# First loads in pieces, later waits for the layer norm's parameters, and a last layer norm shared by ScalarE and VectorE

## The reference

```python
proj = h @ w_in                                   # one combined input projection
a_out = dsa_attention(...)                        # indexer, top-256 keys, latent attention
m_out = mlstm(...)                                # chunkwise matrix memory
mix = concatenate([a_out, m_out]) @ w_out
h = layer_norm(DN_ALPHA * h + mix, ln1_g, ln1_b)
ffn = moe(h, ...)                                 # top-4 of 32 experts, clamped SwiGLU
h = layer_norm(DN_ALPHA * h + ffn, ln2_g, ln2_b)

def layer_norm(x, g, b):
    mu = x.mean(-1, keepdims=True)
    var = square(x - mu).mean(-1, keepdims=True)
    return (x - mu) * rsqrt(var + LN_EPS) * g + b
```

## Time and profile before

| | us |
|---|---|
| median of 3 runs | 2545.79 |
| lowest and highest | 2544.07, 2550.18 |
| the profiled execution, its time | 2546.15 |
| the profiled execution, its span | 2544.3 |
| TensorE busy in the span | 2334.9 (92%) |
| VectorE busy | 1778.5 (70%) |
| ScalarE busy | 1397.7 (55%) |
| GpSimd busy | 301.8 (12%) |

### The profile page before, as it was taken

One profiled execution on the slowest core, in us unless ns is written; L12 is line 12 of the kernel. 1 busy time (PEld: TensorE's weight loads), 2 busy tenths in 40 slices (PEclk: granted clock), 3 DMA queues, 4 the chain that ended last, 5 costly groups with the idle time before them and its releaser, 6 DMA issues.

```text
span 2544.3 us, 37381 instructions
## 1 busy us (share of the span) xinstructions
PE 2334.9 (92%) x10580; PEld 1664.2 (65%) x10581; DVE 1778.5 (70%) x3337; ACT 1397.7 (55%) x2081; POOL 301.8 (12%) x233
## 2 busy tenths in 40 slices
PE   7999998789796699999999999999999999999990
PEld 3544448468453277777777777777777777777770
DVE  0387785446235566787987789787969969778795
ACT  0268624555111155566766577565757757556672
POOL 0000931100200000010011011010001101001002
PEclk9999999799898599999999999999999999999995
DMA  4100002000203356687987789686969969768684
GB/s 165 67 5 33 1 21 96 1 1 1 91 1 141 142 192 217 215 294 230 350 297 260 256 284 360 230 298 213 358 221 324 343 208 352 244 218 293 213 288 155
DMA packets 79981, 488.48 MB, mean 192 GB/s; under 512 B 12019, under 2 KB 13299, under 8 KB 28790
## 3 DMA queue, kind: packets, MB, share of 16 engines
q1 hardware_dynamic: 66512, 449.67, 49.3%
q0 software_dynamic: 11440, 34.10, 6.0%
q10 hardware_dynamic: 1974, 4.02, 0.5%
HBM read 461.91 MB, written 33.29 MB: 195 GB/s over the span
## 4 chain that ended last, share of the span: by engine, by line
PE 71%; DVE 15%; issue 6%; ACT 3%; DVEq 2%; DMA 2%; POOL 0%; POOLq 0%; ACTq 0%; SPq 0%
PE ps L792 9%; PE ps L793 9%; PE ps L794 9%; DVE wlo L1595 8%; PE ps L534 7%; PE ps L789 6%; PE ps L790 6%; PE ps L545 5%; PE ps L713 4%; PE ps L813 3%; PE ps L695 2%; DVEq L380 2%; PE ps L824 1%; PE ps L676 1%; PE ps L563 1%
## 5 line engine op out<-in xcount | busy, mean ns | idle before, releaser
L1595 DVE TENSOR_TENSOR wlo<-raw,whi 128x1024 fp32r<-128x1024 f32 x776 | 932.2, 1220 | 208.3 <-ACT whi L1082 168.2
L1082 ACT ACTIVATE whi<-raw 128x1024 fp32r<-128x1024 f32 x776 | 817.6, 1059 | 405.3 <-PE ps L794 372.3
L792 PE MATMUL ps<-whi,xhi 128*128 128x512 f32 x1024 | 418.0, 408 | 0.0
L793 PE MATMUL ps<-wlo,xhi 128*128 128x512 f32 x1024 | 404.7, 395 | 0.0
L794 PE MATMUL ps<-whi,xlo 128*128 128x512 f32 x1024 | 402.6, 393 | 0.0
L792 PEld LDWEIGHTS ps<-whi,xhi 128*128 128x128 f32 x1024 | 194.3, 190 | 66.6 <-issue 27.6
L794 PEld LDWEIGHTS ps<-whi,xlo 128*128 128x128 f32 x1024 | 195.0, 190 | 42.3
L793 PEld LDWEIGHTS ps<-wlo,xhi 128*128 128x128 f32 x1024 | 195.0, 190 | 36.2
L792 PE MATMUL ps<-whi,hhi 128*128 128x512 f32 x512 | 210.3, 411 | 0.0
L1809 POOL DMA_INDIRECT acc<-ysb,idx_cur x45 | 70.6, 1569 | 1140.5 <-DVE ysb L1644 656.5
L794 PE MATMUL ps<-whi,hlo 128*128 128x512 f32 x512 | 201.4, 393 | 0.0
(11 more groups left out here) (337 smaller groups left out, 3348.5 us busy)
## 6 DMA issues: line engine op xcount, KB each, us to landing
raw<-in_w_gu SPq DMA_DIRECT2D x260, 1024.0 KB, 5.3
raw<-in_w_dn SPq DMA_DIRECT2D x128, 1024.0 KB, 5.1
xT<-in_xT SPq DMA_DIRECT2D x2, 2048.0 KB, 15.7
raw<-in_w_out SPq DMA_DIRECT2D x2, 2048.0 KB, 11.1
h1all<-in_x SPq DMA_DIRECT2D x4, 1024.0 KB, 9.0
hext<-h1all SPq DMA_DIRECT2D x8, 512.0 KB, 11.6
acc<-accst SPq DMA_DIRECT2D x8, 512.0 KB, 2.6
fin<-acc SPq DMA_DIRECT2D x2, 2048.0 KB, 13.3
```

Source lines behind the costliest of these rows:

```text
L792: pe.matmul(bank_ap, hi, whi[:, slot, col, :], start=start, stop=False)
L793: pe.matmul(bank_ap, hi, wlo[:, slot, col, :], start=False, stop=False)
L1082: act.activation(whi[:, j % 2, 2 * g:2 * g + 2, :], raw[:, (j + 2) % 3, 2 * g:2 * g + 2, :], ACT.Copy)\
L1595: dve.tensor_tensor(wlo[:, j % 2, s, :], raw[:, (j + 2) % 3, s, :], whi[:, j % 2, s, :].bitcast(f32), ALU.subtract).then_inc(lo_done, 1)
```

## The change

- The first half of `xT` and slab 0 are loaded in four pieces of two `k` each, alternately, on SP's queue, with a semaphore for each piece (`first_in[0..2]`, and for the last piece `x_in[0]` and `raw_in[0]`). TensorE runs the first half of the query product with `k` outside and `m` inside, four banks open at once, and waits for a piece at every second `k`. It waits for the constants only ahead of the first transpose that uses them. ScalarE's queue issues the constants and the small loads after the first piece has landed.
- TensorE waits for `lnp_in` at the first router product, VectorE at the first use of the first layer norm's scale.
- The last layer norm's scale and shift have buffers of their own, free during the expert loop, and are loaded just ahead of it. `gu` becomes half as large, since its second half was not used, and makes room for one of them.
- `fin` is loaded in four DMAs of two tiles. Tiles 0 and 1 take their statistics on VectorE as before. For tiles 2 to 7 ScalarE sums the row, scales it to minus the mean, sums the squares of the difference, and takes the root. VectorE then does two passes on every tile: (x + minus mean) times scale, and that times the reciprocal root, plus shift. GpSimd does nothing there.

```diff
@@ sync
-            sp.dma_start(xT[:, :, 0:512], a["xT"][:, :, 0:512]).then_inc(x_in[0], 16)
-            slab(0, a["w_qi"])
+            for c in range(4):
+                ks = slice(2 * c, 2 * c + 2)
+                sp.dma_start(xT[:, ks, 0:512], a["xT"][:, ks, 0:512]).then_inc(first_in[c] if c < 3 else x_in[0], 16)
+                sp.dma_start(raw[:, 0, ks, :], a["w_qi"][:, ks, :]).then_inc(first_in[c] if c < 3 else raw_in[0], 16)
...
-            for g in range(2):
-                sp.dma_start(fin[:, 4 * g:4 * g + 4, :],
-                             acc[g * 512:(g + 1) * 512, :].rearrange("(t p) d -> p t d", p=P)).then_inc(fin_in[g], 16)
+            for g in range(4):
+                sp.dma_start(fin[:, 2 * g:2 * g + 2, :],
+                             acc[g * 256:(g + 1) * 256, :].rearrange("(t p) d -> p t d", p=P)).then_inc(fin_in[g], 16)
@@ tensor
-            pe.wait_ge(consts_in, 32)
-            feature_major("qi", 0)
+            for k in range(KT):
+                if k in (0, 2, 4):
+                    pe.wait_ge(first_in[k // 2], 32)
+                elif k == 6:
+                    pe.wait_ge(x_in[0], 16)
+                    slab_ready(0)
+                for m in range(4):
+                    if k == 0:
+                        opened(("qi", m, 0))
+                    ins = pe.matmul(bank(("qi", m, 0))[:, :], raw[:, 0, k, m * P:(m + 1) * P], xT[:, k, 0:512],
+                                    start=k == 0, stop=k == KT - 1)
+                    if k == KT - 1:
+                        closes(ins, ("qi", m, 0))
+            feature_major("qi", 0, [(m, 1) for m in range(4)])
...
             b = opened(("grow",))
+            pe.wait_ge(consts_in, 32)
...
+                if t == 0:
+                    pe.wait_ge(lnp_in, 80)
                 for k in range(KT):
                     ins = pe.matmul(b[0:NE, 0:P], w_rt[:, k, :], h1T[:, t % 2, k, :], start=k == 0, stop=k == KT - 1)
...
-            pe.wait_ge(lnp_in, 80)
             for t in range(NT):
                 mix(t)
@@ scalar
+            act.wait_ge(first_in[0], 32)
             act.dma_start(consts[:, :], a["consts"]).then_inc(consts_in, 16)
...
+            for n in range(2):
+                act.wait_ge(acc_out[n], 8 * NT)
+            act.wait_ge(h_out, 16 * NT)
+            act.dma_start(lnq_g[:, :], a["ln2_g"].partition_broadcast(P)).then_inc(lnq_in, 16)
+            act.dma_start(lnq_b[:, :], a["ln2_b"].partition_broadcast(P)).then_inc(lnq_in, 16)
             with act.Fori(0, n_items) as i:
...
-            piece_split(act, n_items, 1, 3)
-            act.wait_ge(all_added, 1)
             act.wait_ge(bgu_in, n_items * 16 + 16)
-            act.dma_start(lnq[:, 0, :], a["ln2_g"].partition_broadcast(P)).then_inc(lnq_in, 16)
-            act.dma_start(lnq[:, 1, :], a["ln2_b"].partition_broadcast(P)).then_inc(lnq_in, 16)
-            for t in range(NT):
+            for t in range(2):
                 act.wait_ge(f_var, t + 1)
                 act.activation(frs[:, 0, t:t + 1], fmv[:, t, 1:2], ACT.Sqrt, bias=consts[:, C_COL + 1:C_COL + 2])\
                    .then_inc(f_root, 1)
-                act.wait_ge(f_sb, t + 1)
-                act.activation(fin[:, t, :], fin[:, t, :], ACT.Identity, scale=frs[:, 0, t:t + 1],
-                               bias=frs[:, 1, t:t + 1]).then_inc(f_norm, 1)
+            step = serial(act, f_sum)
+            for t in range(2, NT):
+                act.wait_ge(fin_in[t // 2], 16)
+                step(act.activation(fdump[:, :], fin[:, t, :], ACT.Copy, accum_out=fmv[:, t, 0:1]))
+                step(act.activation(frs[:, 1, t:t + 1], fmv[:, t, 0:1], ACT.Copy, scale=-1.0 / D))
+                step(act.activation(fdump[:, :], fin[:, t, :], ACT.Square, bias=frs[:, 1, t:t + 1],
+                                    accum_out=fmv[:, t, 1:2]))
+                act.activation(frs[:, 0, t:t + 1], fmv[:, t, 1:2], ACT.Sqrt, scale=1.0 / D,
+                               bias=consts[:, C_COL + 1:C_COL + 2]).then_inc(f_root, 1)
@@ vector
+                if t == 0:
+                    dve.wait_ge(lnp_in, 80)
                 lstep(dve.tensor_tensor(h1all[:, t, :], h1all[:, t, :], lnp[:, 0, :], ALU.mult))
...
             dve.wait_ge(xres_in, 64)
-            dve.wait_ge(lnp_in, 80)
...
-            for t in range(NT + 2):
-                if t < NT:
-                    dve.wait_ge(fin_in[t // 4], 16)
-                    for n in range(2):
-                        fs(dve.bn_stats(fstat[:, t, n, :], fin[:, t, n * 512:(n + 1) * 512]))
-                    dve.bn_aggr(fmv[:, t, :], fstat[:, t, :, :].rearrange("p a b -> p (a b)")).then_inc(f_var, 1)
...
+            for t in range(2):
+                dve.wait_ge(fin_in[t // 2], 16)
+                for n in range(2):
+                    fs(dve.bn_stats(fstat[:, t, n, :], fin[:, t, n * 512:(n + 1) * 512]))
+                dve.bn_aggr(fmv[:, t, :], fstat[:, t, :, :].rearrange("p a b -> p (a b)")).then_inc(f_var, 1)
+            dve.wait_ge(f_var, 2)
+            for t in range(NT):
                 dve.wait_ge(f_root, t + 1)
                 fs(dve.reciprocal(frs[:, 0, t:t + 1], frs[:, 0, t:t + 1]))
+                mean, op = (fmv[:, t, 0:1], ALU.subtract) if t < 2 else (frs[:, 1, t:t + 1], ALU.add)
+                fs(dve.scalar_tensor_tensor(out=fin[:, t, :], in0=fin[:, t, :], scalar=mean, in1=lnq_g[:, :],
+                                            op0=op, op1=ALU.mult))
+                dve.scalar_tensor_tensor(out=fin[:, t, :], in0=fin[:, t, :], scalar=frs[:, 0, t:t + 1], in1=lnq_b[:, :],
+                                         op0=ALU.mult, op1=ALU.add).then_inc(f_done, 1)
```

More of the change, by code:

```diff
@@ L240, in layer_kernel @@
         tail_ones = at("tail_ones", 57.75, [P, P], bf16)
-        gu = at("gu", X + 92.5, [P, 2, 2, SLAB])
+        gu = at("gu", X + 92.5, [P, 2, SLAB])
         brow = at("brow", X + 134.5, [3, 2 * D], bf16)
@@ L254, in layer_kernel @@
         fin = at("fin", X + 102, [P, NT, D])
-        lnq = at("lnq", X, [P, 2, D])
+        fdump = at("fdump", X, [P, D])
+        lnq_g = at("lnq_g", X + 60, [P, D])
+        lnq_b = at("lnq_b", X + 96.5, [P, D])
         fstat = at("fstat", X + 8, [P, NT, 2, 6])
@@ L312, in layer_kernel @@
         x_in = [sem(f"x_in{n}") for n in range(2)]
+        first_in = [sem(f"first_in{c}") for c in range(3)]
         raw_in = [sem(f"raw_in{n}") for n in range(3)]
@@ L364, in layer_kernel @@
         xg_set, all_added = sem("xg_set"), sem("all_added")
-        fin_in, f_step, f_var, f_root, f_sb, f_norm, f_done, f_out = (
-            [sem(f"fin_in{n}") for n in range(2)], sem("f_step"), sem("f_var"), sem("f_root"), sem("f_sb"), sem("f_norm"),
-            {"dve": sem("f_done_dve"), "pool": sem("f_done_pool")}, sem("f_out"))
-        f_shift = ["dve" if t % 3 == 2 else "pool" for t in range(NT)]
-        f_gain = sem("f_gain")
+        fin_in, f_step, f_var, f_root, f_sum, f_done, f_out = (
+            [sem(f"fin_in{n}") for n in range(4)], sem("f_step"), sem("f_var"), sem("f_root"), sem("f_sum"),
+            sem("f_done"), sem("f_out"))
         last_use = [("qi", 3, 1), ("small", 3), ("qa", 3, 1), ("u", 3, 1), ("v", NT - 1), ("z", NT - 1),
@@ L502, in _ @@
             sp.wait_ge(all_added, 1)
[L503 to L505 removed]
+            for g in range(4):
+                sp.dma_start(fin[:, 2 * g:2 * g + 2, :],
+                             acc[g * 256:(g + 1) * 256, :].rearrange("(t p) d -> p t d", p=P)).then_inc(fin_in[g], 16)
             for t in range(NT):
[L507 removed]
+                sp.wait_ge(f_done, t + 1)
                 sp.dma_start(out[0, t * P:(t + 1) * P, :], fin[:, t, :]).then_inc(f_out, 16)
@@ L1611, in swiglu @@
                 n, uses = gu_place(0, quarter, i, n1, blocks)
-                h, up = hb[:, 0, quarter * 256:(quarter + 1) * 256], gu[:, 0, quarter % 2, 0:256]
+                h, up = hb[:, 0, quarter * 256:(quarter + 1) * 256], gu[:, quarter % 2, 0:256]
                 dve.wait_ge(sig_done[0], c + 1)
@@ L1710, in _ @@
                     item(i, n1, e, ex, (0,))
+            dve.wait_ge(lnq_in, 32)
             fs = serial(dve, f_step)
-            dve.wait_ge(lnq_in, 32)
-            def ln2_finish(t):
+            for t in range(2):
[5 more added lines that the diff above has]
+            for t in range(NT):
                 dve.wait_ge(f_root, t + 1)
                 fs(dve.reciprocal(frs[:, 0, t:t + 1], frs[:, 0, t:t + 1]))
-                dve.scalar_tensor_tensor(out=frs[:, 1, t:t + 1], in0=fmv[:, t, 0:1], scalar=-1.0,
-                                         in1=frs[:, 0, t:t + 1], op0=ALU.mult, op1=ALU.mult).then_inc(f_sb, 1)
-            def ln2_gain(t):
-                dve.wait_ge(f_norm, t + 1)
-                dve.tensor_tensor(fin[:, t, :], fin[:, t, :], lnq[:, 0, :], ALU.mult).then_inc(f_gain, 1)
-            for t in range(NT + 2):
-                if t < NT:
-                    dve.wait_ge(fin_in[t // 4], 16)
-                    for n in range(2):
```

(16 more changed lines are left out.)

1 line of the change is left out of this document (removed).

## The result

| | before | after |
|---|---|---|
| median of the runs beside each other | 2547.98 us (2544.07 to 2551.94, 4 runs) | 2506.97 us (2505.93 to 2507.54, 4 runs) |
| profiled execution | 2546.15 us | 2506.74 us |
| its span | 2544.3 us | 2505.0 us |
| ratio | | 0.9842, 95% interval 0.983 to 0.9855 |

The change makes the kernel 1.6% faster. The forecast was 2509.0, in a range of 2503 to 2518.

The account below looks back on a forecast made before the run. TensorE's chain was taken to bound the kernel, with the layer norm alone setting the end. Gains of 11.0 + 11.0 + 14.8 = 36.8 from 2546.15 gave 2509.4, less 0.4 for the median: 2509.0 us, range 2503 to 2518.

Parts of the forecast that it names:

- Start: First loads: TensorE's first matmul at 6.0 instead of 17.04, since 1.05 MB suffice; a gain of 11.0 us.
- the clock's penalty: Start: the first passes run at 1.2 GHz for about 6.0 us, so the penalty of 3 us comes again.
- no second wait: Start: piece 0 gives TensorE 9.9 us of work while pieces land 2.7 us apart, or 4 to 5 with constants between.
- SP's will now begin near 2.0: Start: SP's queue moves its first bytes near 2.0 instead of 4.4, since ScalarE's loads had gone first.
- Mix: Product waiting for catT instead of the router's bias: begins at about 655.1 in place of 666.15, 11.0 us.
- VectorE's first residual: Mix: its h1all loads, issued from 645.7, land by about 659; the first bank is full at 665, so no wait.
- rival 2: Mix: the clock stays high because TensorE pauses only 2.6 us; 2506.4 us in all, chance 0.12.
- Last layer norm: Tail from the issue of fin to the end: 37.5 us where 52.3 were before, a gain of 14.8 us.
- now again: Tail: the 7.7 us from the last addition to the end of the span were to stay.
- Rival 1: Part of the gain missing, at start and ScalarE's tile (2514.5) or in the mix (2520); together chance 0.15.
- rival 3: No change: ScalarE's copy, square and root need a table load at each switch, 15.4 us, and another term fails; chance 0.02.
- rival 4: Slower: TensorE waits at every second k of its first product and the clock never rises, 2574 in all; chance 0.01.

Follow-up runs that it names:

- the run with the constants at once: Changed kernel without ScalarE's wait for the first piece, so its constant loads are issued at once; 2506.39 us, ratio 0.9852.
- the changed kernel's second trace: The changed kernel run once more, unedited, beside the later experiments; 2506.25 us, ratio 0.9844.
- router's waits alone: Kernel before with only the waits for the first layer norm's parameters moved; 2533.52 us, ratio 0.9951.
- last layer norm alone: Kernel before with only the last layer norm changed: earlier scale and shift loads, four loads of fin, ScalarE's sums; 2528.33 us, ratio 0.9933.
- shift additions on VectorE: Kernel before with all eight tiles' shift additions of the last layer norm on VectorE, none on GpSimd; 2540.69 us, ratio 0.998.
- the run with seven products: Changed kernel with seven products of a zeroed tile on TensorE before the first piece lands; 2503.92 us, ratio 0.9835.
- the other two: Changed kernel with four zero products, 2502.45 us; and with two, five first pieces and a leaner last layer norm, 2498.69 us.
- first loads alone: Kernel before with the first loads in four pieces and nothing else of the change; 2533.96 us, ratio 0.9952.

## Why the prediction was right, and where a term was off

**Start, forecast 11.0 us, measured 9.7.** The mechanism held: 1.05 MB are enough, the clock's penalty comes again, no second wait, and the constants cost nothing. The first piece was ready at 7.30, not 6.0. "SP's will now begin near 2.0" was nearly right in time, yet the rate was not: the prediction used 0.39 MB per us from the first byte on, and the queue had moved 0.16 MB at 3 us, 0.71 at 4.5 and 1.07 at 6. The reason that I gave for the late first byte, that ScalarE's loads go first, is refuted by the run with the constants at once, where the two queues move packets side by side. The penalty of the clock was 0.5 us smaller (5.0 us at the lower level instead of 5.9), which gives the 10.2 us at the 64th pass. That half microsecond is luck: the changed kernel's second trace has 6.1 us, and three traces with the old start (router's waits alone, last layer norm alone, shift additions on VectorE) have 3.2 to 3.5.

**Mix, forecast 11.0, measured 10.8** for the wait; VectorE's first residual, the normalisation of tile 0 and GpSimd's splitting were all in time. The product begins at 647.33, 1.7 us behind the start of the last transposes; I had allowed 0.2 less. On top, the lower level lasted 3.3 us there instead of 5.2. That looks like rival 2 in part, but the runs speak against its reason: with the same short pause the level lasted 6.0 us in the run with the router's waits alone, and in the changed kernel's second trace 5.9. It varies from one execution to the next, and neither the pause nor the change sets it.

**In between, not forecast as a term: 2.2 us lost** to lower clock, as the two stretches show. The prediction had allowed 3 us to both sides for that. In the changed kernel's second trace the way from the 64th pass to the last transposes took 606.7 us, as in the kernel before (606.6), against 608.8 in the first: the loss is no fixed cost of the change.

**Last layer norm, forecast 14.8, measured 19.1.** This is the term that was mis-sized. The 7.7 us "from the last addition to the end of the span", which were to come "now again", are the step that failed: they were GpSimd's drain behind its own last addition, and 4.7 of them left with it. Two runs show it, one adding the drain back by a bare wait, one taking it from the kernel before. The prediction had read that figure without asking which engine it belonged to. The smaller terms: load ready after 4.90 us (forecast 5.5), VectorE's tile 2.71 (2.6, because a fused pass took 1.285 us and not 1.23), ScalarE's tile 2.87 (3.0), one table load of 1.28 us, with the next instruction 0.02 us behind it. VectorE alone set the end; ScalarE was through 4.5 us before it.

**The sum.** 9.7 + 0.5 - 2.2 + 10.8 + 1.4 + 19.1 = 39.3 against 36.8 forecast: two terms too large by 1.5, one too small by 4.3, and the clock near zero in all. So the forecast of 2509.0 came within 2.0 us of 2506.97, partly by luck: the errors had opposite signs, and the kernel before, whose median of 2545.79 the forecast started from, had 2547.98 in the comparison, so that by the medians 41.0 us were saved and not 36.8. Rival 1 (a part of the gain missing), rival 3 (a table load at each switch) and rival 4 (a clock that never rises) did not come: one load, one block of 64 passes.

## What to carry to other kernels

Read the end of a trace engine by engine: an engine whose last work lies late may close later than all others, and what is moved off it there is worth more than its busy time. At the start, cut the first load to what the first passes need, keep other queues' larger packets out of its way, and let TensorE run zeros until it lands; here these brought the first pass 1.7 us forward (the other queue) and the 65th 2.5 and 2.4 us (a first piece of half the size, zeros), and none of them alone stood out in the whole kernel's time. A difference of two or three microseconds at one place is worth checking there, in the trace, since the clock moves the whole kernel's time by as much.

## What the runs showed of the hardware that I had not expected

- GpSimd's closing drain took 7508 ns, whether it came behind a wait, an addition (7.5 of 9.9 us) or its last scatter, in every trace; SyncE's took 12 to 13 ns. Why it is so long stays open.
- Beside another queue's large packets, a queue's first packets came at 4.4 us with a first load of 2048 KB and between 2.5 and 3 with 512 KB, both issued at 0.77. What makes the difference stays open.
- TensorE's clock rose 3.5 us after the first pass on zeros in the run with seven products, and 5.1 and 5.8 us after it in the other two. In the mix it took 3.3 and 5.9 us behind the short pause in two traces of the changed kernel and 6.0 with the router's waits alone, and 5.2, 4.1 and 6.6 behind the long one (kernel before, first loads alone, last layer norm alone). Products of zeros count, and the delay of one and the same kernel differed by 2.6 us between two executions.
